# Scores of the pairs two steps on issued ahead of the values of the current pairs, in a diffusion-transformer inference step

## The reference

```python
s = concat(q @ k_local.T * scale (+ bias), q @ k_ctx.T * scale (, sink))
p = softmax(s)
out = p_local @ v_local + p_ctx @ v_ctx
```

## Time and profile before

| | |
|---|---|
| median of 3 runs | 894.80 us (894.14 to 897.92) |
| the profiled execution | 894.82 us, span 893.0 us |
| busy: PE | 877.5 us, 98% of the span |
| busy: DVE | 706.5 us, 79% |
| busy: ACT | 468.0 us, 52% |
| busy: POOL | 122.3 us, 14% |

### The profile page before, as it was taken

The page is one execution under the profiler, slowest core; times in us unless marked ns, Lnnn a source line. Parts: engine busy times, 40 slices in busy tenths (PEclk is TensorE's granted clock), DMA queues, the critical chain, the costliest instruction groups (busy, mean ns, idle before and its releaser), DMA issues. The chain is left out here.

```text
span 893.0 us, 16552 instructions
## 1 busy us (share of the span) xinstructions
PE 877.5 (98%) x6235; PEld 833.9 (93%) x6235; DVE 706.5 (79%) x1330; ACT 468.0 (52%) x973; POOL 122.3 (14%) x155
## 2 busy tenths in 40 slices
PE   6999999999999999999999999999999999999998
PEld 5689888898889999999998999999999999999997
DVE  4657899799788499774777968997777998778887
ACT  4763444777777533432246734555444555545553
POOL 0000000010000000000000123223333222333221
PEclk9999999999999999999999999999999999999999
DMA  9954344441453220228305478878989886898867
GB/s 366 364 190 166 139 141 143 143 134 62 153 157 117 72 71 1 78 112 328 120 24 214 98 163 188 189 168 195 204 190 201 189 188 164 193 214 188 183 150 146
DMA packets 51663, 145.32 MB, mean 163 GB/s; under 512 B 6000, under 2 KB 12416, under 8 KB 50176
## 3 DMA queue, kind: packets, MB, share of 16 engines
q1 hardware_dynamic: 32000, 102.38, 34.8%
q0 software_dynamic: 18864, 41.11, 24.1%
q10 hardware_dynamic: 720, 0.77, 0.3%
HBM read 121.68 MB, written 12.20 MB: 150 GB/s over the span
## 5 line engine op out<-in xcount | busy, mean ns | idle before, releaser
L1318 ACT ACTIVATE w_hi<-stage 128x512 fp32r<-128x512 f32 (+1 forms) x186 | 106.0, 608 | 98.4 <-DMA stage<-stage 47.8
L2009 DVE TENSOR_TENSOR w_lo<-stage,w_hi 128x512 fp32r<-128x512 f32 (+1 forms) x186 | 117.7, 668 | 25.2 <-ACT w_hi L1318 24.9
L2608 PE MATMUL ps<-m_hi,w_hi 128*128 128x320 f32 x304 | 93.9, 309 | 0.0
L2608 PE MATMUL ps<-m_lo,w_hi 128*128 128x320 f32 x304 | 93.9, 309 | 0.0
L2608 PE MATMUL ps<-m_hi,w_lo 128*128 128x320 f32 x304 | 93.9, 309 | 0.0
L2608 PE MATMUL ps<-h_hi,w_hi 128*128 128x320 f32 x272 | 84.0, 309 | 0.0
L2608 PE MATMUL ps<-h_lo,w_hi 128*128 128x320 f32 x272 | 84.0, 309 | 0.0
L2608 PE MATMUL ps<-h_hi,w_lo 128*128 128x320 f32 x272 | 84.0, 309 | 0.0
L887 ACT ACTIVATE w_hi<-stage 128x1024 fp32r<-128x1024 f32 x47 | 49.6, 1064 | 62.2 <-PE ps L2278 36.9
L2608 PE MATMUL ps<-y_hi,w_hi 128*128 128x320 f32 x264 | 81.7, 309 | 0.0
L2608 PE MATMUL ps<-y_lo,w_hi 128*128 128x320 f32 x264 | 81.6, 309 | 0.0
(11 more groups left out here) (311 smaller groups left out, 2440.0 us busy)
## 6 DMA issues: line engine op xcount, KB each, us to landing
stage<-w_main SPq DMA_DIRECT2D x118, 512.0 KB, 4.3
x<-w_ada SPq DMA_DIRECT2D x21, 512.0 KB, 4.6
stage<-stage POOLq DMA_DIRECT2D x38, 256.0 KB, 4.3
qk<-w_ada SPq DMA_DIRECT2D x7, 1024.0 KB, 12.0
scr<-w_main POOLq DMA_DIRECT2D x28, 256.0 KB, 6.1
y_t<-scr POOLq DMA_DIRECT2D x22, 320.0 KB, 6.5
s_second<-w_main POOLq DMA_DIRECT2D x26, 256.0 KB, 6.2
stage<-w_main POOLq DMA_DIRECT2D x19, 256.0 KB, 6.6
```

Source lines behind the costliest of these rows:

```text
L1318: act.activation(w_hi[:, slot, at:at + job_half(j) * P], left_stage(op, j), ACT.Copy).then_inc(left_hi[op], 1)
L2009: dve.tensor_tensor(w_lo[:, slot, w], left_stage(op, j), w_hi[:, slot, w].bitcast(F32), ALU.subtract).then_inc(left_lo[op], 1)
L2608: ins = pe.matmul(ps[:, BANK_OF[op], 0:TH], wt[:, slot, w], right(op, part, j, k), start=k == 0 and n == 0, stop=k == half - 1 and n == 2)
```

## The change

In the loop over steps on TensorE the two calls of `scores` come ahead of the two calls of `outputs`. Nothing else is changed: the same instructions with the same waits, and no other engine's order.

```diff
                 transposes(b)
                 for chunk in GATE_STEPS[i][n:]:
                     gate_chunk(*chunk)
-                outputs(a)
-                outputs(b)
                 if i + 2 < N_STEPS:
                     scores(a + 4)
                     scores(b + 4)
+                outputs(a)
+                outputs(b)
             pe.wait_ge(ttr_done, 2 * N_PAIRS)
```

## The result

The changed kernel is slower. Over 18 runs each its median is 898.49 us (896.88 to 902.98) against 895.38 us (894.14 to 899.43) before; the ratio is 1.0040 with a 95% interval of 1.0025 to 1.0054, that is 2.2 to 4.8 us.

What follows compares the result with a forecast made beforehand. The prediction took TensorE's instruction stream as the bound. It summed 0.35 us (steps 3 to 6) and 1.14 (steps 9, 13, 16) to 1.49 slower: 894.82 + 1.5 = 896.3 us, range 893.8 to 898.5.

Steps and rivals of the forecast that it cites:

- The bound: Attention stage to the end: TensorE's instruction stream sets the time; what the stage gains or loses there arrives unchanged.
- Part 1: Gaps between kinds of matmul on TensorE, 18 exchanged steps: taken as zero change, bounds 1.8 us either way.
- Rival D: Scores-to-outputs gap costs far more than its neighbours, 0.24 us more in each of 18 steps: 900.6 us, chance 0.05.
- Part 3, the splits: ScalarE's weight splits delay its copies, so second transposes wait in steps 3, 9, 13 and 16.
- the forecast 0.5 to 0.7: Sign of the forecast holding: at step 6 TensorE waits 0.5 to 0.7 us for VectorE, none in front of the outputs.
- The term of 0.38 us: Second transposes behind a split: first head 0.33 us late, second waits 0.05 more; counted three times, 1.14 us.
- Steps 3 to 6: VectorE's delay from step 3 costs TensorE 0.65 us at step 6, whose outputs give back 0.3: net 0.35.
- Part 3, last sentences: GpSimd's (POOL's) copies and SP's late loads come one outputs block earlier; nothing on the path waits for them: no cost.
- One of the prediction's own signs of being wrong: The forecast would be wrong if the attention stage ended over 2 us later.
- Part 2: Scores, some 1.5 us earlier, still find VectorE's row minima done; margin 0.16 us less 0.05, costed at nothing.
- rival C: Scores find minima missing at steps 5 and 6; 0.3 us taken back, up to 0.5 added: 897.1 us, chance 0.10.
- The chance of 0.92: Whole kernel: time stays within 0.5% (4.5 us) of before; slower was given 0.06 and faster 0.02.

Runs made afterwards that it cites:

- experiment 9: Kernel before plus 17 extra, never-read TensorE matmuls of 320 columns behind the attention stage: 897.67 us, ratio 1.0024.
- after_warm: Changed kernel plus two extra, never-read 160-column matmuls ahead of each wait for the second norm's tiles (14 pairs): 899.24 us, ratio 1.0058.
- before_warm: Kernel before plus two extra, never-read 160-column matmuls ahead of each wait for the second norm's tiles (14 pairs): 895.99 us, ratio 1.0019.
- experiment 3: Changed kernel with GpSimd's row copies held until step 3's first transposes and ScalarE's weight split ahead of the output copies: 894.48 us, ratio 0.9987.
- experiment 4: Changed kernel with the new order only in the 13 steps without a weight split on ScalarE: 895.77 us, ratio 0.9998.
- experiment 1: Changed kernel, but GpSimd's two row copies start only behind the first transposes of step 3: 897.62 us, ratio 1.0022.
- experiment 5: Changed kernel with the new order in step 2 alone: stage 127.69 us in one profiled execution, 1.54 more than before.
- experiment 6: Changed kernel with the new order in step 2 alone and GpSimd's row copies as late as before: 895.21 us, stage 126.80, one profiled execution.
- experiment 2: Changed kernel, but ScalarE makes the weight split ahead of the two output copies instead of behind them: 897.91 us, ratio 1.0014.
- experiment 7: Kernel before, old order, but GpSimd's row copies wait for the exponentials of pair 8: 896.18 us, stage 127.91, one profiled execution.

## Why the prediction was wrong

**The bound: right.** TensorE's stream sets the time: 2.51 us added to it raised the lowest run by 2.47 (experiment 9), and the 2.54 us lost in the stage by as much (`after_warm` against `before_warm`).

**Part 1, the gaps between kinds: right.** The change of the gaps was taken as zero. The new gap, scores to outputs, is 0.20, 0.25 and 0.31 us for a last part of 128, 192 and 256 columns, as the scores-to-transposes gap was before, and experiments 3 and 4 leave nothing for 18 exchanges. Rival D falls.

**Part 3, the splits: right in place and mechanism, a little small.** The waits for the copies stand in steps 3, 9, 13 and 16. (The largest wait in the view, 0.4 us for a copy, is that of step 6, and it is VectorE's: its first scaling there ended at 212.34 + 0.49 = 212.83, and the transposes followed at 212.97, 0.15 later as in the kernel before, where they followed 212.01 at 212.15. This wait was 0.26 before and 0.41 now, not the forecast 0.5 to 0.7, because TensorE came later itself.) The term of 0.38 us measured 0.46: the first head's 0.34 was forecast as 0.33, and the second head's wait is 0.12 instead of 0.05. Three times 0.08 is 0.24 us. Steps 3 to 6 without GpSimd cost 0.65 gross, as summed. Step 6 gave back 0.3, as forecast.

**Part 3, last sentences: the step that failed.** "POOL's copies and SP's late loads wait for scores, and these come one outputs block earlier, which nothing on the path waits for." The term was put at nothing. It is true that nobody on the path waits for GpSimd's results. The cost was the other kind: what GpSimd runs beside. The row of 191.94 would have told when its work starts, and the VectorE rows next to it that a 1.24 us shift puts it on the scalings of pair 7. I priced the engine by its waiters and not by its neighbours. The missing term is 0.86 to 0.89 us (experiments 1, 5 and 6; 0.64 where the split is ahead). Together with the small terms it makes 1.49 + 0.19 + 0.86 = 2.54: the 0.19 are 0.24 from the three splits, less what steps 3 to 6 cost below their 0.35. One of the prediction's own signs of being wrong came true by it: the stage took over 2 us longer.

**Part 2 and rival C: half right.** The scores do find their minima missing, in steps 3 (0.5 us) and 5 (0.3), but because VectorE was pushed back by GpSimd and not because the place is too early: in experiment 1, where the scalings are back at 0.75, no score waits in either step. At 6 the margin held in both. That this rival was priced near the measured loss (897.1, 2.3 us over before) is luck: it named steps 5 and 6, and another cause.

**The range and the chances.** The room above the forecast was there for the unknown gap, which turned out to cost nothing, and not for this. That its top, 898.5, lies at the median is luck too, more so as the kernel before has a median of 895.38 now, 0.56 above the base of the forecast. The chance of 0.92 for a change within 0.5% fits a ratio of 1.0040, though the interval ends at 1.0054. (By the prediction's own parts, slower by more was 0.05 + 0.025, not 0.06.)

## What to carry to other kernels

When a producer is moved forward, list everyone who waits for its semaphore, also those off the critical path, and look in the timeline at what their work will then run beside: an engine that nobody waits for can still hold up its neighbour. And when a consumer is moved back, look at what stands behind it in the queue of the engine that takes its result: here a weight split of 0.94 us had been free only because the moved block covered it, and putting it ahead of the waiting instruction made it free again.

## What the runs showed of the hardware

A VectorE scaling of 128x384 float32 within SBUF (`tensor_scalar`) takes 0.41 us by itself. One that started while GpSimd copied or cleared SBUF lasted until a GpSimd instruction had ended, and ended 0.21 to 0.22 us behind it: nine scalings in four profiles (the changed kernel, experiments 2, 5 and 7), with 1.00 to 2.09 us each. The pair took 3.15 us where 0.75 is usual, in the old order of TensorE too (2.27 and, for a pair of which one was hit, 1.32). GpSimd's memset alone did it as well: the scaling of 197.75 in experiment 7 met nothing else, and took 1.00 us. The row minima (L1610), which read one operand from PSUM and one from SBUF, ran beside the same GpSimd work at their usual 0.67 us.

The Trainium skill (SBUF — State Buffer, Who interferes with whom) says that VectorE shares a pair of SBUF ports with GpSimd, that `tensor_scalar` in a two-port mode takes it for the whole instruction, and that the one that issues second is fully blocked. The trace agrees in the blocking: the end of the second scaling followed the end of the memset (192.08 + 0.95 = 193.03) by 0.2 us. It doesn't agree in the order. That scaling started at 191.15, 0.9 us ahead of the memset by the profile (whose spans on GpSimd are rough), and still ended behind it, while in experiment 2 the scaling went first. The rule would have turned "earlier" into a cost, had the rows of GpSimd been laid beside those of VectorE.
